# First block's projections as three single-pass products, norms from raw sums by token, last layer on 512 columns

## The reference

```
# first block, one layer
mod = silu(c) @ w_ada + b_ada            # 6 x 1024, in 12 units of 512 columns
h = rms_norm(x, g1) * (1 + scale1) + shift1
x_m, o_pre, gates, a_q, a_k, a_v = split(h @ w_in)
y = concat(mlstm_mixer(x_m, o_pre, gates, ...), dilated_attention_mixer(a_q, a_k, a_v, ...))
x = x + gate1 * (y @ w_out)
h2 = rms_norm(x, g2) * (1 + scale2) + shift2
x = x + gate2 * expert_choice_ffn(h2, ...)          # 16 experts
# second block
h = layer_norm(concat(meta, x))                      # "norm E"
for l in range(2):
    mix = concat(retention, pool, forgetting_attention)(h @ w_in[l])
    h = layer_norm(ALPHA * h + mix @ w_out[l])                             # norm 0
    h = layer_norm(ALPHA * h + (silu(h @ w1[l]) * (h @ w3[l])) @ w2[l])    # norm 1
return h[:, 16:]                                     # the meta tokens are dropped
```

## Time and profile before

| | |
|---|---|
| median of 3 runs | 3158.36 us (3158.31 to 3165.85) |
| the profiled execution | 3158.13 us |
| its span | 3156.4 us |
| PE busy | 2827.6 us (90%) |
| PE weight loads busy | 1980.9 us (63%) |
| DVE, ACT, POOL busy | 958.2, 646.4, 115.9 us |
| share of the chain that ended last: PE, DVE, ACT | 84%, 10%, 4% |
| experts | 604 to 1596 us |

### The profile page before, as it was taken

How to read it: one execution, slowest core, us unless ns; L and a number is a source line. 1 busy time by engine, 2 the same in 40 slices (tenths; PEclk the granted TensorE clock), 3 DMA queues, 4 the chain that set the end, 5 groups by cost and what they waited for, 6 DMA issues and landing times.

```text
span 3156.4 us, 39370 instructions
## 1 busy us (share of the span) xinstructions
PE 2827.6 (90%) x17108; PEld 1980.9 (63%) x17108; DVE 958.2 (30%) x1564; ACT 646.4 (20%) x1118; POOL 115.9 (4%) x125
## 2 busy tenths in 40 slices
PE   6987778599999999999979988999998988899997
PEld 3433553434333433433458857999998776799996
DVE  3026652311111111111162253423234243423323
ACT  1021441100100100010032142322223223321222
POOL 0000010000000000000000320000000050000000
PEclk8997889599999999999989869999999987999999
DMA  9234002199999999999911101223241110133321
GB/s 324 81 133 157 24 1 82 48 418 417 414 406 417 413 408 418 417 405 418 394 47 61 34 27 54 73 77 105 79 104 37 51 61 14 55 89 92 94 82 46
DMA packets 245291, 558.59 MB, mean 177 GB/s; under 512 B 36817, under 2 KB 198995, under 8 KB 220204
## 3 DMA queue, kind: packets, MB, share of 16 engines
q1 hardware_dynamic: 233584, 548.48, 45.6%
q0 software_dynamic: 1552, 5.70, 0.6%
q10 hardware_dynamic: 10028, 2.53, 0.4%
HBM read 552.46 MB, written 4.23 MB: 176 GB/s over the span
## 4 chain that ended last, share of the span: by engine, by line
PE 84%; DVE 10%; ACT 4%; issue 2%; DMA 0%; ACTq 0%; DVEq 0%; POOL 0%
PE vpsum L1825 20%; PE vpsum L1725 14%; PE apsum L1825 11%; PE vpsum L1742 7%; PE apsum L1709 4%; PE apsum L1834 3%; PE vpsum L1530 3%; PE vpsum L1767 2%; PE vpsum L1662 2%; PE apsum L1767 2%; PE apsum L1854 1%; PE apsum L1784 1%; PE vpsum L1967 1%; PE vpsum L1591 1%; PE vpsum L1605 1%
## 5 line engine op out<-in xcount | busy, mean ns | idle before, releaser
L1725 PE MATMUL vpsum<-ring,arena 128*64 128x512 f32 x2048 | 449.3, 597 | 0.8 <-ACT arena L839 0.8
L1825 PE MATMUL apsum<-stream_r,wring_r 128*128 128x264 f32 x2880 | 369.7, 289 | 15.9 <-DVE stream_r L1284 15.9
L1825 PEld LDWEIGHTS apsum<-stream_r,wring_r 128*128 128x128 f32 x2880 | 362.3, 193 | 19.1 <-issue 16.4
L1825 PE MATMUL vpsum<-work_r,wring_r 128*128 128x264 f32 x2880 | 353.7, 285 | 3.3 <-DVE work_r L1408 3.3
L1825 PEld LDWEIGHTS vpsum<-work_r,wring_r 128*128 128x128 f32 x2880 | 353.0, 189 | 3.4 <-issue 3.4
L1312 DVE TENSOR_TENSOR wring_r<-wring,wring_r 128x2048 fp32r<-128x2048 f32 (+3 forms) x100 | 207.2, 2076 | 407.1 <-ACT wring_r L879 407.1
L1725 PEld LDWEIGHTS vpsum<-ring,arena 128*64 128x64 f32 x2048 | 144.9, 138 | 291.3 <-issue 291.3
L1825 PE MATMUL vpsum<-stream_r,wring_r 128*128 128x264 f32 x2400 | 302.5, 286 | 10.5 <-DVE body L1395 10.5
L1825 PEld LDWEIGHTS vpsum<-stream_r,wring_r 128*128 128x128 f32 x2400 | 297.7, 191 | 10.9 <-DVE body L1395 10.9
L879 ACT ACTIVATE wring_r<-wring 128x2048 fp32r<-128x2048 f32 (+3 forms) x100 | 172.8, 1730 | 621.2 <-DMA wring<-w_ffn 600.9
L1742 PE MATMUL vpsum<-ring,arena 128*64 128x512 f32 x1024 | 226.8, 595 | 11.0 <-ACT arena L851 11.0
(11 more groups left out here) (394 smaller groups left out, 2707.2 us busy)
## 6 DMA issues: line engine op xcount, KB each, us to landing
ring<-w_gate SPq DMA_DIRECT2D x64, 2048.0 KB, 16.4
ring<-w_up SPq DMA_DIRECT2D x64, 2048.0 KB, 8.7
ring<-w_down SPq DMA_DIRECT2D x64, 2048.0 KB, 12.3
wring<-w_ffn SPq DMA_DIRECT2D x88, 512.0 KB, 4.7
ring<-w_ada SPq DMA_DIRECT2D x12, 2048.0 KB, 9.0
wring<-w_ffn SPq DMA_DIRECT2D x32, 704.0 KB, 4.6
ring<-w_in SPq DMA_DIRECT2D x5, 2048.0 KB, 23.2
wring<-w_in SPq DMA_DIRECT2D x10, 1024.0 KB, 5.4
```

The costliest lines, as they stand in the source:

```text
L1725: last = pe.matmul(banks[g][CAP * blk:CAP * blk + CAP, :], xin[:, 2 * r + c, :], w[:, at:at + 512], start=r + c == 0, stop=r + c == 4)
L1825: last = pe.matmul(b[:, k, 0:HW], w_[:, c, col:col + P], halves(x[:, c, :])[:, k, :].bitcast(FR), start=c == 0 and i == 0, stop=c == chunk ...
```

## The change

**First block.** The five projections and the output projection become three single-pass products each, of float32r parts. Five times ACT copies a unit into the high part (`input_high`), POOL subtracts (`input_low`); of w_out POOL does both, in its loop over heads. The stream's high part (`f_hi`) is made by ACT, the low part (`f_lo`) by DVE. The gates come first, then q, k, v, xm, o. Modulation rows 4 to 7 stand within o, rows 8 to 11 in the attention, at query tiles 1, 5, 9 and 13 (`MOD_ROW_AT`). A table gives each load its slot and what it waits for.

```diff
+        LOADS = [*((f"ada{i}", 3 + i, None) for i in range(4)), ("in0", 7, None), ("in1", 4, row_used(1)), ("in2", 6, row_used(3)),
+                 ("in3", 8, q_used), ("in4", 5, k_used), ("ada4", 7, v_used), ("ada5", 7, row_used(4)), ("ada6", 4, xm_used), ("ada7", 8, xm_used),
+                 ("ada8", 3, o_used), ("ada9", 5, o_used), ("ada10", 6, o_used), ("ada11", 7, row_used(5)), ("out0", 4, row_used(6)), ("out1", 8, row_used(7))]
...
+        HIGH_SLOT = [place % NSLOT for place in (8, 5, 7, 4, 6)]
+        HIGH_FREE = [None, row_used(2), q_used, k_used, v_used]
+        OUT_HIGH_SLOT, OUT_HIGH_FREE = [place % NSLOT for place in (3, 5)], [row_used(8), row_used(9)]
...
-            for n, (src, _, _) in enumerate(units):
-                if n >= NSLOT:
-                    _, used, count = units[n - NSLOT]
-                    sp.wait_ge(used, count)
-                sp.dma_start(slot(n), src).then_inc(loaded[n % NSLOT], 16)
+            for name, _, free in LOADS:
+                if free is not None:
+                    sp.wait_ge(*free)
+                sp.dma_start(chunks(ring[:, SLOT_OF[name], :]), load_source(name)).then_inc(loaded[SLOT_OF[name]], 16)
```

POOL, with the loop over the attention's heads:

```diff
+            def input_low(i):
+
+                pool.wait_ge(in_high, i + 1)
+                k = SLOT_OF[f"in{i}"]
+                pool.tensor_tensor(ring_r[:, k, :].bitcast(FR), ring[:, k, :], ring_r[:, HIGH_SLOT[i], :], ALU.subtract).then_inc(in_low, 1)
...
+            for i in (Q_W, K_W, V_W):
+                input_low(i)
...
+            load_hankel(0)
+            input_low(XM_W)
+            input_low(O_W)
             for h in range(AH):
                 if h >= 1:
                     pool.wait_ge(v_filled, V.count(f"toep{h - 1}"))
-                pool.dma_start(hankel[:, 0, 0:896], bass.AP(bvec_d.tensor, bvec_d.offset + h * DIFFS, [[1, P], [1, 896]])).then_inc(hankel_in, 16)
+                    load_hankel(h)
+                i, k = h // 4, h % 2
+                at, words = SLOT_OF[f"out{i}"], slice(2048 * k, 2048 * k + 2048)
+                src, high, low = ring[:, at, words], ring_r[:, OUT_HIGH_SLOT[i], words], ring_r[:, at, words]
+                if h % 4 < 2:
+                    pool.wait_ge(loaded[at], 16 * NTH[f"out{i}"])
+                    pool.wait_ge(*OUT_HIGH_FREE[i])
+                    pool.tensor_copy(high.bitcast(FR), src).then_inc(out_high, 1)
+                else:
+                    pool.wait_ge(out_high, 2 * i + 2)
+                    pool.tensor_tensor(low.bitcast(FR), src, high, ALU.subtract).then_inc(out_low, 1)
```

ACT:

```diff
+            def input_high(i):
+
+                at = SLOT_OF[f"in{i}"]
+                act.wait_ge(loaded[at], 16 * NTH[f"in{i}"])
+                if HIGH_FREE[i] is not None:
+                    act.wait_ge(*HIGH_FREE[i])
+                act.activation(ring_r[:, HIGH_SLOT[i], :].bitcast(FR), ring[:, at, :], ACT.Copy).then_inc(in_high, 1)
...
+            input_high(Q_W)
+            act.wait_ge(dve_const, 9)
+            wg_src = w_in[:, :, 1024:1040].rearrange("p c (d k h) -> p c k d h", d=2, k=2)
...
+                act.wait_ge(h_done, c + 1)
+                act.activation(f_hi[:, c, :].bitcast(FR), hT[:, c, :], ACT.Copy).then_inc(h_high, 1)
+            input_high(K_W)
```

DVE, between the chunks of hT, and PE's product:

```diff
+            def stream_low(c):
+                dve.wait_ge(h_high, c + 1)
+                dve.wait_ge(h_used, c + 1)
+                dve.tensor_tensor(f_lo[:, c, :].bitcast(FR), hT[:, c, :], f_hi[:, c, :], ALU.subtract).then_inc(h_low1, 1)
+
             for c in range(KC):
                 dve.tensor_scalar(hT[:, c, :], hT[:, c, :], g1s[:, c:c + 1], mod[:, c:c + 1], ALU.mult, ALU.add).then_inc(h_done, 1)
-            for c in range(MH):
```

```diff
+            def terms1(w, x, c, m):
+
+                cols = slice(P * m, P * m + P)
+                return ((w[0][:, c, cols], x[0][:, c, :]), (w[0][:, c, cols], x[1][:, c, :]), (w[1][:, c, cols], x[0][:, c, :]))
+
+            def dense(b, w, x, m, done):
 
                 for c in range(KC):
-                    last = pe.matmul(b[:, :], w[:, c, col:col + P], hT[:, c, :], start=c == 0, stop=c == KC - 1)
+                    for i, (w_, x_) in enumerate(terms1(w, x, c, m)):
+                        last = pe.matmul(b[:, :], w_.bitcast(FR), x_.bitcast(FR), start=c == 0 and i == 0, stop=c == KC - 1 and i == 2)
                 last.then_inc(done, 1)
...
+            w = inputs(Q_W)
+            dense_by_chunk([vclaim("aqT", m) for m in range(4)], w, stream, v_filled, lambda c: pe.wait_ge(h_low1, c + 1), range(KC))
+            w = inputs(K_W)
+            for m in range(4):
+                dense(vclaim("akT", m), w, stream, m, v_filled)
```

```diff
+                b = plan.take(dve, apair, a_filled, f"tok{k}", 0)[:, 0, :]
+                minus, second, square, var, std = (tokst[:, i, 0:t] for i in range(5))
+                dve.tensor_scalar(minus, b[:, 0:t], -1.0 / D, None, ALU.mult).then_inc(tok_mean, 1)
+                link2(dve.tensor_scalar(second, b[:, 8:8 + t], 1.0 / D, None, ALU.mult))
+                dve.wait_ge(tok_mean, n + 1)
+                link2(dve.tensor_tensor(square, minus, minus, ALU.mult))
+                link2(dve.tensor_tensor(var, second, square, ALU.subtract))
+                dve.tensor_scalar(var, var, 0.0, None, ALU.max).then_inc(a_freed, 1)
+                dve.wait_ge(tok_std, n + 1)
+                dve.reciprocal(second, std).then_inc(tok_rstd, 1)
+                dve.wait_ge(a_freed, plan.count(f"mean{k}"))
+                for c in range(4):
+                    center(c)
+                dve.wait_ge(a_freed, plan.count(f"rstd{k}"))
+                scale(0)
                 for c in range(KC):
-                    dve.tensor_tensor(src[:, c, :], src[:, c, :], mu, ALU.subtract).then_inc(centered, 1)
-                dve.wait_ge(a_freed, plan.count(var_stage))
-                link2(dve.reciprocal(rstd, rstd))
-                for c in range(KC):
-                    dve.scalar_tensor_tensor(H[:, c, :], src[:, c, :], gain[:, c:c + 1], rstd, ALU.mult, ALU.mult).then_inc(scaled, 1)
-                    if bias is not None and c >= 2:
-                        stream_low(c - 2)
-                if bias is not None:
-                    stream_low(KC - 2)
-                    stream_low(KC - 1)
+                    if c + 1 < KC:
+                        scale(c + 1)
+                    if bias is not None:
+                        stream_low(c)
```

```diff
+            def strips(b, src, chunks, ready, whole=False):
+
+                for c in chunks:
+                    ready(c)
                     q = 32 * (c % 4)
-                    for k in range(2):
-                        last = pe.matmul(b[q:q + 32, k, 0:HW], ones[:, 0:32], halves(src[:, c, :])[:, k, :], start=c < 4, stop=c >= 4)
-                last.then_inc(a_filled, 1)
...
+            def first_moments(plan, k, src, squares, n, ready, whole=False):
+
+                sums = plan.claim(pe, apair, a_freed, f"sum{k}", 0)
+                strips(sums, src, range(4), ready, whole)
+                squared = plan.claim(pe, apair, a_freed, f"sq{k}", 0)
+                strips(squared, squares, range(4), squares_ready(n), whole)
+                return sums, squared
...
+                strips(squared, squares, range(7, 8), squares_ready(n), whole).then_inc(a_filled, 1)
+                b = plan.claim(pe, apair, a_freed, f"tok{k}", 0)[:, 0, :]
+                for at, part, stage in ((0, mu, f"sum{k}"), (8, rstd, f"sq{k}")):
+                    pe.wait_ge(a_freed, plan.count(stage))
+                    for i in range(t):
+                        x0 = min(P * i, L2 - P)
+                        last = pe.matmul(b[:, at + i:at + i + 1], part[:, x0:x0 + P], inv32[:], start=True, stop=True)
+                last.then_inc(a_filled, 1)
+                for row, ready_row, stage in ((0, tok_mean, f"mean{k}"), (1, tok_rstd, f"rstd{k}")):
+                    b = flat(plan.claim(pe, apair, a_freed, stage, 0))
+                    pe.wait_ge(ready_row, n + 1)
+                    for i in range(t):
+                        x0 = max(0, P * i - S + P - META) if i == TT else 0
+                        last = pe.matmul(b[:, P * i:min(P * i + P, L2)], tokst[:, row, i:i + 1].broadcast_to([P, P]), ident[:, x0:P], start=True, stop=True)
```

```diff
+            def columns(b, x, whole):
+
+                return [(b[:, 0, :], x[:, 0:S])] if whole else [(b[:, k, 0:HW], halves(x)[:, k, :]) for k in range(2)]
...
-                def project(b, w, col, hi, lo, ready=None):
+                def project(b, w, col, hi, lo, ready=None, whole=False):
...
                             ready(c)
                         for i, (w_, x) in enumerate(terms(w, hi, lo)):
-                            for k in range(2):
-                                last = pe.matmul(b[:, k, 0:HW], w_[:, c, col:col + P], halves(x[:, c, :])[:, k, :].bitcast(FR),
+                            for dst, x_ in columns(b, x[:, c, :], whole):
```

(21 more changed lines are left out.)

577 lines of the change are left out of this document (345 added, 232 removed).

## The result

Four runs of the changed kernel took 3051.46 to 3066.49 us, median 3063.12; beside them the kernel before took 3157.91 to 3165.85, median 3158.34. The ratio is 0.9687, with a 95% interval of 0.9657 to 0.9716: 95 us or 3.1% faster, where 142 us were forecast. 3063 lies outside the range of 2984 to 3044. The profiled execution took 3062.95 us, its span is 3060.8.

A forecast was written before the change was run, and what follows sets the result against it. PE was taken as full in the FFN stretches, with gaps round the norms and behind DVE before the attention. Front, attention and mix -49, norms -46.2, last layer -47 took 3158.1 to 3016 us, range 2984 to 3044.

The forecast's parts named there:

- The price of a product of 512 columns: Projections, output projection and last layer: a single-pass 512-column product costs 216 to 224 ns, taken as 216.
- Rival B: 512-column products cost 224.4 ns, over 2448 products: +21 us, 3037 us; chance 0.12.
- POOL's lows: First block's projections: low parts take 9.3 us a unit, hidden under the 20.7 us of a projection.
- norm E: Norm between experts and second block: gap falls from 32.0 to 19.7 us, a gain of 12.3 us.
- q's start: Front: the first q product at 86 us, behind the gate loads and the stream's high part near 73 us.
- Rival A: Front: the gate loads stay at 5 us each, q starts 26 us later, 3042 us; chance 0.15.
- The stall for hankel(1): Attention, head 1: its load queues on POOL behind the copy of w_out's first unit, +16.4 us.
- rival C: Attention: no stall for hankel(1), as w_out's unit lands early or POOL passes it, 2998 us; chance 0.17.
- Layer 0's first norm: Second block: the norm's gap falls from 27.2 to 16.6 us, a gain of 10.6 us.
- rival D: All norms: they give half the forecast gain, 3039 us; chance 0.08.
- Rival E: 512-column products: the 193 ns weight load is not hidden, 406 ns a product, +465 us, 3481 us; chance 0.03.
- rival F: 512-column products cost 242 ns, gate loads stay slow, norms keep their hops: 3152 us, no change; chance 0.02.

The follow-up runs named there:

- Experiments 4: Changed kernel with the last layer computing its 528 columns in two halves again: median 3090.46 us, ratio to before 0.9775.
- 5: Changed kernel with the last layer's second of three terms computed for 384 of 512 columns only, output incomplete: 3029.39 us in one run.
- Experiment 9: Changed kernel with POOL beginning the subtraction of xm's weights only when the gates' scans are over: median 3059.65 us.
- 10: Changed kernel with the low parts of the second block's first three units made by DVE instead of POOL: median 3060.53 us.
- 11: Changed kernel plus 14 unused DVE subtractions of 1024 words beside k's products: 3077.28 us in one run.
- experiment 1: Changed kernel with POOL splitting w_out from head 3 on, each head's bias matrix loaded ahead of that: median 3052.52 us, ratio to before 0.9658.
- 6: Changed kernel with the last layer's gate and up products reading columns at multiples of 512 words, output of other data: 3068.48 us in one run.
- experiment 2: Changed kernel with POOL's whole-unit subtractions cut into pieces of 512 words: median 3061.22 us.
- 7: Changed kernel with the four o products ahead of modulation rows 4 to 7: median 3068.02 us, ratio to before 0.9702.

## Why the prediction was wrong

I compare trace with trace: 3060.8 us of span, and 3014 by my sum.

**The price of a product of 512 columns.** This is the step that failed most: "I take 216, since the over of a 512-column record is 2.5". That was the fp32 record, which takes twice the time a column. The single-pass rows stood in the earlier trace rows, and I used them only for an upper end that took their 11.1 ns as fixed. The last layer's products cost 231.1 ns, outside the 216 to 224 that I had called both sides: 1776 x 15.1 = 26.8 us. From the start of layer 1's w_out to the end of its last product the traces have 459.9 before (2661.94 is in its chain) and 429.9 after, -30.0, where my terms give -57.6: of the 27.6 between them this one term is all but 0.8. In the first block the same product took 226.7 ns, 10.7 over my 216: q, k, o and the output projection, 480 of the 672 products there, lie on the chain and make 5.1 us more. The term is some 32 of the 47 us. Experiments 4 and 5 show it: 384 columns lie on the line through 264 and 512. Had I scaled the row by columns, 121.1 x 512/264 = 234.9, the forecast would have been 4 ns too high instead of 15 too low. Rival B named the cause and took too small a size (224.4 ns). The 2.5 ns gap that I had quoted from the Trainium skill ("TensorE: Matmul & The Clock Gate", "Back-to-back issue gap") is not what float32r shows here at any of three widths: 11, 14 and 18 ns over the columns at full clock. The section gives that formula for a single product, and for a stream of loads and products some 131 ns at 512 columns; the trace has neither.

**DVE's chain and POOL.** "POOL's lows take 9.3 us a unit, under the 20.7 of a projection, so they hide". They hide from PE and not from DVE. A subtraction on POOL held a scan for 8.9 us and a norm step for 5.9 in the front, and the residuals of norm E for some 6.5. Experiment 9 takes the first hold away by moving POOL's instruction alone, 10 takes the last away by giving the work to DVE, 11 makes one by accident. The Trainium skill has the rule ("SBUF — State Buffer", "Who interferes with whom"): a VectorE instruction with two SBUF inputs and a GpSimd one that reads SBUF want one port pair, and the second to come is blocked until the first ends. The traces agree: scans, norm steps, residuals and subtractions on two SBUF tensors waited, reciprocals and copies out of PSUM beside the same subtractions kept their 3.3 and 0.7 us. I should have asked of each DVE step how many of its inputs lie in SBUF; but that count is not the whole of it, since the copy in experiment 1 reads one SBUF tensor and was held too. The scans and norm steps that I put beside V and XM are, with the holds, the bound from 130 to 194.6 us, where I had o begin at 180. So the first toep came 12.6 us later than forecast (-56.4 for -69), and norm E with its first products gave 4.6 for 12.3.

**What was right.** q's start (84.4 for 86), by the terms given: the gate loads, the small vectors, then f_hi. That it came so close is part luck: with the quick pair of gate loads it would have been 79.5. Rival A, gate loads at 5 us each and q 26 us later, fell. The stall for hankel(1): 17.3 us in experiment 1, 16.4 forecast; rival C fell. From the first toep to the output projection the traces have +29.5, forecast +33.4 (with the 0.8 of the later start). The output projection itself took 12.0 less, forecast 13.4; its 192 products at 226.7 ns instead of 216 make 2.1 us. Layer 0's second norm 7.0 (7.2). Layer 0's first norm gave 7.7 for 10.6: its chain of 12.4 us is the 12.6 of the forecast, but the products on both sides were slower than counted, the first 240 records of w_out 30.91 us for 29.1 at a granted clock of 0.94, and the FFN's first 192 26.1 for 23.3 at 0.90. The end gave 8.1 for 5.5. All norms together gave some 38 of the 46.2, so rival D, the half, fell.

**The sum of the misses**: front, attention and mix +10.1 (-38.9 for -49), router and experts -1.4, norm E with the raw products +7.7, from there to layer 0's w_out +2.0, layer 0's norm and FFN +4.9, to layer 1's w_out -1.7, layer 1 +27.6, the end -2.6: +46.6 of 47.

**Rival E**, the slow side, did not come: a product of 512 columns costs 231 ns and not the 274 from which it decides, so the weight load of 193 ns lies beside it. With the price and the norms as measured, rival F fell too.

**Not settled.** Why a single-pass column costs 0.44 to 0.45 ns at a granted clock of 1.00, and why the same product costs 226.7 ns in the first block and 231.1 in the last layer. DVE's traffic is not it (11), nor a row start at multiples of 512 words (6), though the place changed the price by up to 1.6%. Both were tried in one place only, DVE's traffic in the first block and the row starts in the last layer. Open too is why the scan of experiment 2 waited for all eight pieces, while a norm step got in between two, and why the copy of experiment 1 was held.

## What to carry to other kernels

Price an instruction from a row of its own type and scale it by size; a constant taken from another type of pass is no bound. Before giving work to an idle POOL, look at what DVE does in those microseconds: here one instruction of 9 us on POOL stopped one of DVE's for up to 8.9 us, and where DVE is on the path that is not free. A wait that is hidden now becomes the next bound as soon as its cover goes: look for loads that share a slot, and ask what is asked for only when the one before has been used.

## What the runs showed of the hardware

POOL's subtraction of 128x4096 takes 9.03 us, and a DVE scan of 8x512 that starts with it 10.1 us instead of 1.2; cut in eight, POOL still holds the scan for the whole series, but another step only for 0.1 us. float32r products cost 121.1, 174 and 231.1 ns at 264, 384 and 512 columns.

The mixer's stage, the same instructions, took 92.1 us in the changed kernel's trace and 95.6 in experiment 2's, with a mean granted clock of 0.83 and 0.80. The two windows, of the changed kernel and of experiment 2:

```profile
368.24:460.35 92.11, 63.57 (x273) 44.27 (x273) 57.62 (x195) 42.05 (x134) 9.35 (x32) 0.83 0.00 1
```

```profile
357.56:453.15 95.59, 66.91 (x273) 46.70 (x273) 57.67 (x195) 42.03 (x134) 9.35 (x32) 0.80 0.00 1
```

DVE and ACT are busy as long in both; PE's products are 3.3 us longer. Over the changed kernel and the twelve experiments this stage took 92.1 to 97.2 us, at a clock of 0.83 down to 0.78. The output projection behind it took 45.2 and 46.7 us, and to the experts' first product the kernels of experiments 2 and 7 lost 3 us more. So 3 to 8 us of a change in the front can be given back or won by the clock that PE is granted behind it; what sets it for the same instructions, no run here shows.
